# Expert stage of a streaming encoder trunk: gathered rows copied ahead of the tanh, the shared down-projection bank by bank, the last expert's products ahead of a weight conversion

## The chip, the cores and the metric

The kernel runs on one core of one Trainium2 chip. The metric is the device time of one execution in microseconds (us), the median over the runs. The core's engines work side by side, each through its own list of instructions in order: TensorE (PE: matrix products, with its weight loads as PEld), VectorE (DVE), ScalarE (ACT), GpSimd (POOL, almost unused here) and SyncE (SP, which issues the DMA transfers of the weights). They wait for one another by semaphores.

## The reference

Two layers of an encoder trunk run over 320 tokens (256 of a prompt, 64 of a sample), width 1024. What matters here is the second half of each layer, a mixture of experts; everything before it (attention, mLSTM, gated MLP, merge, first layer norm) is untouched.

```python
def _swiglu(x, wg, wu, wd):
    return (jax.nn.silu(x @ wg) * (x @ wu)) @ wd

def _moe(x, router_w, router_b, wg, wu, wd, sg, su, sd):
    ...                                   # s = sigmoid router; best group of 4 experts, best 2 in it
    out = _swiglu(xf, sg, su, sd)         # shared expert, all 320 tokens
    for e in range(N_EXPERTS):            # 16 experts, hidden width 256
        out = out + gate[:, e:e + 1] * _swiglu(xf, wg[e], wu[e], wd[e])
    return out
```

Each layer then ends with a layer norm of `DN_ALPHA * x + moe_out`. All values are f32.

## The kernel before

**Weights.** All weights come as blocks of 128 x 1024 f32 (512 KB), numbered through both layers. SP loads block n into one of 8 raw buffers (`w32`, L424). ACT rounds it to f16, `hi_at` (L545, writes `whi`), and DVE takes the rest, `lo_at` (L1034, writes `wlo`); both have 4 slots. So every product is made of three f16 products (whi by hi, whi by lo, wlo by hi), summed in PSUM. `hi_at(n)` waits until PE is done with block n-4 (`blk_done`), `lo_at(n)` waits for `hi_at(n)` (`hi_done`), PE's product waits for `lo_at(n)` (`ready`, `lo_done`), and SP's load of block n+8 waits for `lo_at(n)` as well.

**Expert stage.** The tokens of a group of 4 experts are gathered into 128 columns, so that an expert works on 128 columns and not on 320. For each of the 16 experts e (4 groups of 4; e2 is its parity) the engines do this, all written out by hand in this order:
- PE (L2190 to L2213): four blocks of 24 matmuls, j = 0 to 3 (gate half 0, up half 0, gate half 1, up half 1), into the banks `UPB[2*e2]` and `UPB[2*e2+1]`. After j = 0 come the two matmuls that spread the expert's gate values (L2137, L2139), after j = 1 come the 12 matmuls of `gather` (L2160) that fetch a quarter of the next group's rows into bank 5. UPB is the banks 1, 2, 3, 0 in this order, so even experts use 1 and 2, odd ones 3 and 0.
- ACT (L945 to L961): `hi_e(1)`, `hi_e(2)`, tanh of the gate halves (L950), `hi_e(3)`, the copy of the gathered rows out of bank 5 into `x_grp` (L955), `hi_e(4)`, and the f16 rounding of the hidden values (L960), which waits for DVE's products of this expert (`e_prod`). `hi_e(j)` converts block g0+3+j, where g0 is the expert's first block.
- DVE (L1631 to L1652): `lo_e(1)`, `lo_e(2)`, `lo_e(3)`; then the three products: (1 + tanh) by gate (L1636, waits for the tanh), by up (L1640, frees the expert's two banks: `e_free`), by the expert's gate values (L1644, `e_prod`); then `lo_e(4)` and the low part of the hidden values (L1649, waits for L960, signals `e_lo`).

At a group's start PE makes a small product for the way back (L2190, bank 7), ahead of which it waits until the copies of the previous group's four gathers are done (`xg_ev`), and ACT copies its result (L936) ahead of `hi_e(1)`.

**Down stage.** Once the experts are done PE runs `down` (L2150) for the shared expert's first half of the output: 24 matmuls of 320 columns over banks 0, 1, 2, 3, after a wait for the last expert's `e_free`. Its signal `blk_done` lets ACT convert the fourth block after it. Then `group_down` (L2233) makes 24 matmuls of 512 columns for each of 4 groups; its first waits for the last expert's `e_lo`. `scatter` (L2249) brings the results back to token order, and the same follows for the output's second half.

Of the kernel before, what the change touches and what calls it, by code (L numbers as in the profile page):

```python
# [35 lines left out]
ACT = mybir.ActivationFunctionType  # L36
# [3 lines left out]
P = 128  # L40
DM, L = 1024, 2
TP, TS, PAST = 256, 64, 256
T = TP + TS
# [49 lines left out]
def slot(l, n):  # L93
    return (l * NB + n) % SLOTS
# [23 lines left out]
def build_trunk(nc, d):  # L118
    with ExitStack() as ctx:
# [416 lines left out]
        def _(act):  # L536
# [48 lines left out]
            for l in range(0, L):  # L585
# [331 lines left out]
                with act.If(fits):  # L917
# [14 lines left out]
                    for gg in range(0, GROUPS // 2):  # L932
                        for g2 in range(2):

                            act.wait_ge(ot_ps.sem, ot_ps.value(l, gg * 2 + (g2 + 1)))
                            A(slot_tok[:, bass.ds((gg * 2 + g2) * T, T)], bank[7][:, 0:T], ACT.Copy,  # L936
                              scale=1 / (UN * XS)).then_inc(ot_ev.sem, 1)
                            for qq in range(0, 2):
                                for e2 in range(2):
                                    e = gg * 8 + qq * 2 + (4 * g2 + e2)  # L940
                                    g0 = e * 4 + (U0 + 4)

                                    def hi_e(j):
                                        hi_at(l, g0 + (j + LEAD))

                                    hi_e(1)
                                    hi_e(2)
                                    act.wait_ge(blk_done.sem, blk_done.value(l, g0 + 3))
                                    act.wait_ge(e_free.sem, e_free.value(l, e))
                                    A(ht[:, 0:2 * CAP], bank[UPB[2 * e2]][:, 0:2 * CAP], ACT.Tanh,  # L950
                                      scale=UN / 2).then_inc(e_tanh.sem, 1)
                                    hi_e(3)

                                    act.wait_ge(xg_ps.sem, xg_ps.value(l, e + 5))
                                    A(f16_b[:, bass.ds(qq * 1024 + (e2 * 512 + HEND + (1 - g2) * 2048),  # L955
                                                       512)], bank[5][:, :], ACT.Copy
                                      ).then_inc(xg_ev.sem, 1)
                                    hi_e(4)
                                    act.wait_ge(e_prod.sem, e_prod.value(l, e + 1))
                                    A(hhi[:, bass.ds(e * (2 * CAP) + H0, 2 * CAP)], h2[:, 0:2 * CAP],  # L960
                                      ACT.Copy, scale=UN * UN * XS / (2 * GS)).then_inc(e_hi.sem, 1)  # L961
# [65 lines left out]
        def _(dve):  # L1027
# [82 lines left out]
            for l in range(0, L):  # L1110
# [500 lines left out]
                with dve.If(fits):  # L1611
# [11 lines left out]
                    for ee in range(0, EXPERTS // 2):  # L1623
                        for e2 in range(2):
# [3 lines left out]
                            def lo_e(j):  # L1628
                                lo_at(l, g0 + (j + LEAD))

                            lo_e(1)  # L1631
                            lo_e(2)
                            lo_e(3)

                            dve.wait_ge(e_tanh.sem, e_tanh.value(l, e + 1))
                            V.scalar_tensor_tensor(h1[:, 0:W2], ht[:, 0:W2], 1.0,  # L1636
# [7 lines left out]
                            V.tensor_tensor(two(h2[:, 0:W2]), two(h1[:, 0:W2]),  # L1644
                                            bank[4 + 2 * e2][:, 0:CAP].unsqueeze(1).broadcast_to(
                                                [P, 2, CAP]), ALU.mult).then_inc(e_prod.sem, 1)
                            lo_e(4)
                            dve.wait_ge(e_hi.sem, e_hi.value(l, e + 1))
                            V.scalar_tensor_tensor(hlo[:, bass.ds(e * W2 + H0, W2)], h2[:, 0:W2],  # L1649
# [59 lines left out]
        def _(pe):  # L1709
# [16 lines left out]
            def ready(l, n):  # L1726

                pe.wait_ge(lo_done.sem, lo_done.value(l, n + 1))
# [52 lines left out]
            for l in range(0, L):  # L1781
# [385 lines left out]
                with pe.If(fits):  # L2167
# [85 lines left out]
                                a.then_inc(sums.sem, 1)  # L2253

                    pe.wait_ge(u_lo.sem, u_lo.value(l, 2))
                    pe.wait_ge(e_free.sem, e_free.value(l, EXPERTS))
                    down(l, D0, slot(l, D0), half0, 0, True, False)
                    for gg in range(0, GROUPS // 2):
                        for g2 in range(2):
                            group_down(gg * 2 + g2, g2, 0)  # L2260
# [201 lines left out]
```

## Time and profile before

| | us |
|---|---|
| median of 3 runs | 1105.39 (1103.49 to 1106.1) |
| profiled execution, its own time | 1105.55 |
| span of that execution, first to last instruction | 1103.3 |
| PE busy | 1031.3 (93%) |
| DVE busy | 835.9 (76%) |
| ACT busy | 659.2 (60%) |
| mean granted TensorE clock | 0.984 |

The profile describes one execution. Busy times are sums over the whole span; a stage has its own limit, so the expert stage has to be read from its own stretch. It lies at about 375 to 487 us in the first layer and 919 to 1029 us in the second. A row of the timeline gives an instruction's start (us from the span's start) and duration; an instruction may start shortly before the one ahead of it on its engine has ended. In square brackets stands how long the engine was idle before it and what ended that.

### The profile page before, as it was taken

The numbers are of one execution on the slowest core, as the hardware profiler recorded it, in microseconds if no ns is written. First come the engines' busy times: TensorE is split into PE (matmuls) and PEld (weight loads), VectorE is DVE, ScalarE is ACT, GpSimd is POOL, SyncE is SP. The second block draws the span as 40 slices with busy tenths as digits, with TensorE's granted clock in tenths as the row PEclk, the third lists the DMA queues.
The fourth block names the chain that finished last, engine by engine and source line by source line (L and its number), as shares of the span: only waits on it lengthen the run. The fifth ranks groups of instructions, "written<-read, shape, count | busy, mean of one in ns | idle before, by whom it ended". The sixth has DMA issues, their size and how long they took to land. (4 is left out here: it accounts for less than half of the span.)

```text
span 1103.3 us, 24810 instructions
## 1 busy us (share of the span) xinstructions
PE 1031.3 (93%) x10206; PEld 790.6 (72%) x10206; DVE 835.9 (76%) x1500; ACT 659.2 (60%) x1059; POOL 0.7 (0%) x10
## 2 busy tenths in 40 slices
PE   6999999999998799999999999999999888999994
PEld 4877777777775699965467777777777567999442
DVE  4786768654878699988987766676559777999886
ACT  5655545654345777777667445556533567777763
POOL 0000000000000000000000000000000000000000
PEclk9999999999999899999999999999999999999998
DMA  9744343323552389988725433442243415999861
GB/s 350 274 151 156 123 155 118 115 97 124 191 167 75 114 294 324 333 305 305 267 89 190 151 129 136 139 140 93 97 152 136 147 46 166 329 329 326 322 230 50
DMA packets 59655, 205.08 MB, mean 186 GB/s; under 512 B 7088, under 2 KB 10348, under 8 KB 59020
## 3 DMA queue, kind: packets, MB, share of 16 engines
q1 hardware_dynamic: 55980, 195.96, 51.2%
q10 hardware_dynamic: 3552, 7.42, 1.9%
q8 instruction: 85, 1.39, 0.5%
q14 instruction: 38, 0.31, 0.1%
HBM read 198.77 MB, written 3.40 MB: 183 GB/s over the span
## 5 line engine op out<-in xcount | busy, mean ns | idle before, releaser
L1034 DVE SCALAR_TENSOR_TENSOR wlo<-w,whi 128x1024 f16<-128x1024 f32 x358 | 429.7, 1221 | 83.5 <-ACT whi L545 81.9
L545 ACT ACTIVATE whi<-w 128x1024 f16<-128x1024 f32 x358 | 370.3, 1049 | 81.8 <-PE bank L1718 51.3
L1718 PE MATMUL bank<-xhi,whi 128*128 128x320 f16 x704 | 211.3, 300 | 0.0
L1718 PE MATMUL bank<-xlo,whi 128*128 128x320 f16 x704 | 210.8, 299 | 0.0
L1718 PE MATMUL bank<-xhi,wlo 128*128 128x320 f16 x704 | 210.7, 299 | 0.0
L1718 PE MATMUL bank<-arena_b,whi 128*128 128x128 f16 x2048 | 181.0, 220 | 0.0
L1718 PE MATMUL bank<-arena_b,wlo 128*128 128x128 f16 x1024 | 176.8, 220 | 0.0
L1718 PEld LDWEIGHTS bank<-arena_b,whi 128*128 128x128 f16 x2048 | 158.4, 98 | 0.0
L1718 PEld LDWEIGHTS bank<-arena_b,wlo 128*128 128x128 f16 x1024 | 100.8, 98 | 0.0
L1718 PEld LDWEIGHTS bank<-xhi,whi 128*128 128x128 f16 x704 | 68.9, 98 | 30.5 <-issue 2.5
L1718 PEld LDWEIGHTS bank<-xhi,wlo 128*128 128x128 f16 x704 | 69.0, 98 | 26.9
L1718 PEld LDWEIGHTS bank<-xlo,whi 128*128 128x128 f16 x704 | 69.0, 98 | 26.3 <-issue 1.4
L1741 PE MATMUL bank<-whi,xhi 128*128 128x128 f16 (+1 forms) x384 | 66.4, 220 | 0.0
L1741 PE MATMUL bank<-wlo,xhi 128*128 128x128 f16 (+1 forms) x384 | 66.0, 219 | 0.0
L1741 PE MATMUL bank<-whi,xlo 128*128 128x128 f16 (+1 forms) x384 | 66.0, 219 | 0.0
L1718 PE MATMUL bank<-br_hi,whi 128*128 128x320 f16 x192 | 57.4, 299 | 0.0
L1718 PE MATMUL bank<-br_lo,whi 128*128 128x320 f16 x192 | 57.4, 299 | 0.0
L1718 PE MATMUL bank<-br_hi,wlo 128*128 128x320 f16 x192 | 57.4, 299 | 0.0
L2233 PE MATMUL bank<-whi,arena_a 128*128 128x512 f16 x128 | 48.6, 379 | 1.8 <-DVE wlo L1034 1.8
L2233 PE MATMUL bank<-wlo,arena_a 128*128 128x512 f16 x128 | 48.5, 379 | 0.0
L2233 PE MATMUL bank<-whi,arena_b 128*128 128x512 f16 x128 | 48.5, 379 | 0.0
L689 ACT ACTIVATE arena_a<-bank,par_h 128x320 f32<-128x320 f32 x24 | 12.7, 527 | 58.6 <-PE bank L1718 58.6
(353 smaller groups left out, 1770.8 us busy)
## 6 DMA issues: line engine op xcount, KB each, us to landing
w<-in_w SPq DMA_DIRECT2D x358, 512.0 KB, 4.7
arena_b<-head_rows ACTq DMA_DIRECT2D x2, 1920.0 KB, 7.7
xT<-in_x SPq DMA_DIRECT2D x2, 640.0 KB, 4.8
out_y<-xT SPq DMA_DIRECT2D x4, 320.0 KB
rows<-in_rows ACTq DMA_DIRECT2D x1, 1024.0 KB, 11.4
rows<-in_rows SPq DMA_DIRECT2D x1, 1024.0 KB, 5.8
out_ckv<-arena_a SPq DMA_DIRECT2D x2, 320.0 KB
acc<-kr SPq DMA_DIRECT2D x2, 288.0 KB
```

The lines of the kernel that those rows point to most:

```text
L545: A(whi[:, n % SLOTS, :], w32[:, n % RAW, :], ACT.Copy, scale=WS).then_inc(hi_done.sem, 1)
L689: A(dst, bank[(M0 + step) % 4][:, 0:T], func, scale=scale, bias=par_t[:, bass.ds(col, 1)]).then_inc(z_ev.sem, 1)
L1034: V.scalar_tensor_tensor(wlo[:, n % SLOTS, :], w32[:, n % RAW, :], WS, whi[:, n % SLOTS, :], ALU.mult, ALU.subtract).then_inc(lo_done.sem, 1)
L1718: ins = M(out, w[:, s, sub * P:(sub + 1) * P], rhs(part, k), start=(n == 0), stop=(n == 3 * len(subs) - 1))
L1741: ins = M(bank[b][0:m, i * P:(i + 1) * P], x[:, k, t0:t0 + m], w[:, s, k * P:(k + 1) * P], start=(j == 0), stop=(j == 3 * KD - 1))
L2233: a = M(b[:, :], h_[:, bass.ds(g * (8 * CAP) + ((2 * q + kt) * CAP + H0), CAP)], w[:, slot(l, n), kt * 512:(kt + 1) * 512], start=(q == 0 ...
```

## The change

Three edits, all in the branch where every group's tokens fit into 128 columns (the one that runs here):
- ACT: the copy of the gathered rows (L955) moves from behind `hi_e(3)` to ahead of the tanh (L950), for each of the 16 experts.
- DVE: for the last expert only, `lo_e(3)` moves from ahead of the three products to behind them.
- PE: the shared expert's first `down` starts after a wait for the free banks of expert 14 only, does all six matmuls of bank 1, then of bank 2, then waits for the last expert's `e_free` and does banks 3 and 0. It was both halves of the depth over banks 0, 1, 2, 3. The 24 products are the same.

```diff
@@ -945,16 +945,15 @@
 
                                     hi_e(1)
                                     hi_e(2)
+                                    act.wait_ge(xg_ps.sem, xg_ps.value(l, e + 5))
+                                    A(f16_b[:, bass.ds(qq * 1024 + (e2 * 512 + HEND + (1 - g2) * 2048),
+                                                       512)], bank[5][:, :], ACT.Copy
+                                      ).then_inc(xg_ev.sem, 1)
                                     act.wait_ge(blk_done.sem, blk_done.value(l, g0 + 3))
                                     act.wait_ge(e_free.sem, e_free.value(l, e))
                                     A(ht[:, 0:2 * CAP], bank[UPB[2 * e2]][:, 0:2 * CAP], ACT.Tanh,
                                       scale=UN / 2).then_inc(e_tanh.sem, 1)
                                     hi_e(3)
-
-                                    act.wait_ge(xg_ps.sem, xg_ps.value(l, e + 5))
-                                    A(f16_b[:, bass.ds(qq * 1024 + (e2 * 512 + HEND + (1 - g2) * 2048),
-                                                       512)], bank[5][:, :], ACT.Copy
-                                      ).then_inc(xg_ev.sem, 1)
                                     hi_e(4)
                                     act.wait_ge(e_prod.sem, e_prod.value(l, e + 1))
                                     A(hhi[:, bass.ds(e * (2 * CAP) + H0, 2 * CAP)], h2[:, 0:2 * CAP],
@@ -1630,7 +1629,8 @@
 
                             lo_e(1)
                             lo_e(2)
-                            lo_e(3)
+                            if e < EXPERTS - 1:
+                                lo_e(3)
 
                             dve.wait_ge(e_tanh.sem, e_tanh.value(l, e + 1))
                             V.scalar_tensor_tensor(h1[:, 0:W2], ht[:, 0:W2], 1.0,
@@ -1644,6 +1644,8 @@
                             V.tensor_tensor(two(h2[:, 0:W2]), two(h1[:, 0:W2]),
                                             bank[4 + 2 * e2][:, 0:CAP].unsqueeze(1).broadcast_to(
                                                 [P, 2, CAP]), ALU.mult).then_inc(e_prod.sem, 1)
+                            if e == EXPERTS - 1:
+                                lo_e(3)
                             lo_e(4)
                             dve.wait_ge(e_hi.sem, e_hi.value(l, e + 1))
                             V.scalar_tensor_tensor(hlo[:, bass.ds(e * W2 + H0, W2)], h2[:, 0:W2],
@@ -2253,8 +2255,17 @@
                                 a.then_inc(sums.sem, 1)
 
                     pe.wait_ge(u_lo.sem, u_lo.value(l, 2))
-                    pe.wait_ge(e_free.sem, e_free.value(l, EXPERTS))
-                    down(l, D0, slot(l, D0), half0, 0, True, False)
+                    pe.wait_ge(e_free.sem, e_free.value(l, EXPERTS - 1))
+                    ready(l, D0)
+                    for b in UPB:
+                        if b == UPB[2]:
+                            pe.wait_ge(e_free.sem, e_free.value(l, EXPERTS))
+                        for kt in range(2):
+                            for w, h_ in ((whi, hhi), (whi, hlo), (wlo, hhi)):
+                                a = M(bank[b][:, 0:T], w[:, slot(l, D0), (4 * kt + b) * P:(4 * kt + b + 1) * P],
+                                      h_[:, kt * T:(kt + 1) * T], start=(kt == 0 and w is whi and h_ is hhi),
+                                      stop=False)
+                    a.then_inc(blk_done.sem, 1)
                     for gg in range(0, GROUPS // 2):
                         for g2 in range(2):
                             group_down(gg * 2 + g2, g2, 0)
```

ACT, a group's first expert, before. `bank7` is the small product's, `bank1` the gate halves' and `bank5` the gather's; `whi<-w32` are the conversions `hi_e`:

```order
L936 ACTIVATE arena_a<-bank7 128x320 [waits ot_ps]
L545 ACTIVATE whi<-w32 128x1024 [waits blk_done,loaded5]
L545 ACTIVATE whi<-w32 128x1024 [waits blk_done,loaded6]
L950 ACTIVATE mq<-bank1 128x256 [waits e_free,blk_done]
L545 ACTIVATE whi<-w32 128x1024 [waits blk_done,loaded7]
L955 ACTIVATE arena_b<-bank5 128x512 [waits xg_ps]
L545 ACTIVATE whi<-w32 128x1024 [waits blk_done,loaded0]
L960 ACTIVATE arena_a<-mo 128x256 [waits e_prod]
```

And now:

```order
L936 ACTIVATE arena_a<-bank7 128x320 [waits ot_ps]
L545 ACTIVATE whi<-w32 128x1024 [waits blk_done,loaded5]
L545 ACTIVATE whi<-w32 128x1024 [waits blk_done,loaded6]
L949 ACTIVATE arena_b<-bank5 128x512 [waits xg_ps]
L954 ACTIVATE mq<-bank1 128x256 [waits e_free,blk_done]
L545 ACTIVATE whi<-w32 128x1024 [waits blk_done,loaded7]
L545 ACTIVATE whi<-w32 128x1024 [waits blk_done,loaded0]
L959 ACTIVATE arena_a<-mo 128x256 [waits e_prod]
```

The copy out of bank5 stands ahead of the tanh, and two conversions now stand in a row behind the tanh. It is so for all 16 experts.

DVE, the last expert, from the last product of expert 14 on, before (`wlo<-w32,whi` are the conversions `lo_e`, x3 three in a row):

```order
L1644 TENSOR_TENSOR mo<-mk,bank4 128x256 [waits gb_ps]
L1034 SCALAR_TENSOR_TENSOR wlo<-w32,whi 128x1024 [waits hi_done]
L1649 SCALAR_TENSOR_TENSOR arena_b<-mo,arena_a 128x256 [waits e_hi]
L1034 SCALAR_TENSOR_TENSOR wlo<-w32,whi 128x1024 [waits hi_done] x3
L1636 SCALAR_TENSOR_TENSOR mk<-mq,bank3 128x256 [waits e_tanh]
L1640 TENSOR_TENSOR mk<-mk,bank0 128x256 [waits blk_done]
L1644 TENSOR_TENSOR mo<-mk,bank6 128x256 [waits gb_ps]
L1034 SCALAR_TENSOR_TENSOR wlo<-w32,whi 128x1024 [waits hi_done]
L1649 SCALAR_TENSOR_TENSOR arena_b<-mo,arena_a 128x256 [waits e_hi]
```

And now:

```order
L1644 TENSOR_TENSOR mo<-mk,bank4 128x256 [waits gb_ps]
L1033 SCALAR_TENSOR_TENSOR wlo<-w32,whi 128x1024 [waits hi_done]
L1651 SCALAR_TENSOR_TENSOR arena_b<-mo,arena_a 128x256 [waits e_hi]
L1033 SCALAR_TENSOR_TENSOR wlo<-w32,whi 128x1024 [waits hi_done] x2
L1636 SCALAR_TENSOR_TENSOR mk<-mq,bank3 128x256 [waits e_tanh]
L1640 TENSOR_TENSOR mk<-mk,bank0 128x256 [waits blk_done]
L1644 TENSOR_TENSOR mo<-mk,bank6 128x256 [waits gb_ps]
L1033 SCALAR_TENSOR_TENSOR wlo<-w32,whi 128x1024 [waits hi_done] x2
L1651 SCALAR_TENSOR_TENSOR arena_b<-mo,arena_a 128x256 [waits e_hi]
```

One conversion has moved from the three ahead of the products to the one behind them; the low part of the hidden values is still last.

PE, the first product of the shared down-projection, from its first matmul on, before:

```order
L2150 MATMUL bank0<-arena_a,whi 128x320 [waits lo_done,e_free,u_lo]
L2150 MATMUL bank0<-arena_b,whi 128x320
L2150 MATMUL bank0<-arena_a,wlo 128x320
L2150 MATMUL bank1<-arena_a,whi 128x320
L2150 MATMUL bank1<-arena_b,whi 128x320
L2150 MATMUL bank1<-arena_a,wlo 128x320
L2150 MATMUL bank2<-arena_a,whi 128x320
L2150 MATMUL bank2<-arena_b,whi 128x320
L2150 MATMUL bank2<-arena_a,wlo 128x320
```

And now, with the rows that only repeat left out:

```order
L2265 MATMUL bank1<-arena_a,whi 128x320 [waits lo_done,e_free,u_lo]
L2265 MATMUL bank1<-arena_b,whi 128x320
L2265 MATMUL bank1<-arena_a,wlo 128x320
L2265 MATMUL bank1<-arena_a,whi 128x320
...
L2265 MATMUL bank2<-arena_a,whi 128x320
...
L2265 MATMUL bank3<-arena_a,whi 128x320 [waits e_free]
...
L2265 MATMUL bank3<-arena_a,wlo 128x320
```

The wait for `e_free` is for one expert fewer at the first matmul, and a second one stands at bank3, twelve matmuls later.

## Rows read from the trace of the kernel before

**Rows 1.** Waits over the whole span: total us, times, longest us.

```profile
PE bank L2190 <- ACT arena_b L955: 5.5, 6, 0.9
...
PE bank L2150 <- issue: 5.2, 2, 2.6
```

**Rows 2.** Stretches: us, busy time of each engine, PEclk, DMA share, GB/s.

```profile
375.90:382.40 6.50, 5.12 (x50) 4.86 (x48) 4.03 (x7) 3.74 (x5) 0.00 (x0) 0.50 0.35 96
404.50:430.30 25.80, 24.87 (x443) 24.73 (x444) 24.54 (x33) 20.27 (x30) 0.00 (x0) 1.00 0.93 329
481.00:487.00 6.00, 3.41 (x25) 2.47 (x26) 4.30 (x7) 2.14 (x4) 0.00 (x0) 1.00 0.89 320
487.00:508.00 21.00, 21.00 (x101) 9.61 (x99) 19.60 (x19) 18.26 (x20) 0.00 (x0) 1.00 0.87 326
```

**Rows 3.** Timeline of DVE, expert 1 of the first layer.

```profile
389.23 3.50 DVE L1034 SCALAR_TENSOR_TENSOR wlo<-w,whi 128x1024 f16<-128x1024 f32 x3
392.65 0.41 DVE L1636 SCALAR_TENSOR_TENSOR mk<-mq,bank 128x256 f32<-128x256 f32 x1
...
393.65 0.42 DVE L1644 TENSOR_TENSOR mo<-mk,bank 128x256 f32<-128x256 f32 x1
393.99 1.22 DVE L1034 SCALAR_TENSOR_TENSOR wlo<-w,whi 128x1024 f16<-128x1024 f32 x1
```

**Rows 4.** Timeline of ACT, same expert, until its hidden values are rounded.

```profile
387.84 0.42 ACT L960 ACTIVATE arena_a<-mo 128x256 f16<-128x256 f32 x1 [1.20 <-DVE mo L1644]
388.16 1.99 ACT L545 ACTIVATE whi<-w 128x1024 f16<-128x1024 f32 x2
390.05 0.36 ACT L950 ACTIVATE mq<-bank 128x256 f32<-128x256 f32 x1
390.32 1.05 ACT L545 ACTIVATE whi<-w 128x1024 f16<-128x1024 f32 x1
391.26 0.58 ACT L955 ACTIVATE arena_b<-bank 128x512 f16<-128x512 f32 x1
391.74 1.05 ACT L545 ACTIVATE whi<-w 128x1024 f16<-128x1024 f32 x1
394.10 0.42 ACT L960 ACTIVATE arena_a<-mo 128x256 f16<-128x256 f32 x1 [1.31 <-DVE mo L1644]
```

**Rows 5.** All instructions of line 1636, the first product of each expert, both layers.

```profile
L1636 DVE SCALAR_TENSOR_TENSOR mk<-mq,bank x32: 410/414/416, 386.4 to 1025.1; 128x256 f32<-128x256 f32 x32
```

**Rows 6.** Timeline of ACT, tanh of the first layer's first expert.

```profile
383.88 0.38 ACT L950 ACTIVATE mq<-bank 128x256 f32<-128x256 f32 x1 [1.75 <-PE bank L1718]
```

**Rows 7.** Timeline of ACT at the start of the second group (expert 4).

```profile
406.95 0.42 ACT L936 ACTIVATE arena_a<-bank 128x320 f16<-128x320 f32 x1
407.27 1.99 ACT L545 ACTIVATE whi<-w 128x1024 f16<-128x1024 f32 x2
409.66 0.38 ACT L950 ACTIVATE mq<-bank 128x256 f32<-128x256 f32 x1 [0.40 <-PE bank L1718]
```

**Rows 8.** Timeline of DVE, third low conversion of expert 4.

```profile
411.02 1.23 DVE L1034 SCALAR_TENSOR_TENSOR wlo<-w,whi 128x1024 f16<-128x1024 f32 x1 [0.31 <-ACT whi L545]
```

**Rows 9.** Timeline of DVE, end of expert 14 and expert 15, first layer.

```profile
475.17 1.22 DVE L1034 SCALAR_TENSOR_TENSOR wlo<-w,whi 128x1024 f16<-128x1024 f32 x1
476.31 0.41 DVE L1636 SCALAR_TENSOR_TENSOR mk<-mq,bank 128x256 f32<-128x256 f32 x1
...
483.06 0.42 DVE L1640 TENSOR_TENSOR mk<-mk,bank 128x256 f32<-128x256 f32 x1
...
485.05 0.42 DVE L1649 SCALAR_TENSOR_TENSOR arena_b<-mo,arena_a 128x256 f16<-128x256 f32 x1
```

**Rows 10.** Timeline of PE, first matmul of the shared product and of group_down.

```profile
483.59 0.30 PE L2150 MATMUL bank<-arena_a,whi 128*128 128x320 f16 x1 [2.59 <-issue]
...
486.84 0.38 PE L2233 MATMUL bank<-whi,arena_a 128*128 128x512 f16 x1
```

**Rows 11.** Issues of weight loads at 481 to 487 us: count, KB, median us to landing.

```profile
w<-in_w SPq DMA_DIRECT2D x3, 512.0 KB, 5.8
```

## Prediction, made before the changed kernel ran

> **What bounds the kernel now.** I read the waits first. PE, busy for 93% of the span, waits at each group's start for the copy of the last gather, 0.9 us each, 5.5 us in all six times, and 2.6 us in each layer ahead of the shared down product [rows 1]. Those are the waits that the three edits aim at, some 10.7 us in all. Whether they can be had depends on what paces the stretch between them, so I then read the stretches: over one group's 25.8 us PE is busy 24.87 us and DVE 24.54 us, ACT 20.27 us [rows 2]. PE and DVE are too close to be told apart by busy time, and PE's own work of at most 24.87 / 4 = 6.22 us per expert has to be held against DVE's order of work. So I went to DVE's timeline of one inner expert. Its first product starts at 392.65 [rows 3], that of the expert ahead at 386.4 [rows 5]: 6.27 us apart, and DVE never waits. The pieces fill it: three low conversions from 389.23 on, 1.14 us apart, products, the fourth conversion at 393.99. So **DVE sets the pace** inside a group at 6.27 us per expert, PE keeps up with a little to spare, and PE's 0.9 us at a group's start is partly that slack.
>
> ACT has idle time too, but it lies in one place: 1.31 us ahead of the rounding of the hidden values, where it waits for DVE's last product [rows 4]. Between that rounding and the third conversion ACT doesn't stop: rounding at 387.84, two conversions from 388.16, tanh at 390.05, third conversion from 390.32 to 391.37. DVE's third low conversion needs that result. The three end at 389.23 + 3.50 = 392.73, so the third starts 1.22 us earlier, at 391.51 [rows 3]. How soon after its release it can start is seen at expert 4: the tanh starts at 409.66, the conversion behind it 0.27 us later and ends after 1.05, at 410.98 [rows 4, 7], and DVE starts at 411.02 [rows 8], so 0.03 us. **The slack between ACT's third conversion and DVE's is therefore 391.51 - 391.37 - 0.03 = 0.11 us.** This is the number on which the prediction rests.
>
> **Edit 1, the copy ahead of the tanh.** It adds no work, but puts the copy on the way from the rounding to the third conversion. What it costs there is its distance to the next instruction on ACT, 391.26 to 391.74, 0.48 us [rows 4]. 0.11 us of that is covered; 0.37 us is not. And the delay isn't paid once: DVE's product then comes later, ACT's rounding waits for it and starts its next round later. The ring, from an expert's last product (L1644) to that of the next: product to rounding 0.45 [rows 3, 4], rounding to first conversion 0.32, two conversions to the next instruction 1.89, copy 0.48, tanh to third conversion 0.27, the conversion 1.05 [rows 4], release 0.03, third low conversion to first product 1.14 (475.17 to 476.31 [rows 9]), first to last product 1.00 (392.65 to 393.65 [rows 3]). Sum **6.63 us**; without the copy it was 6.15, under DVE's 6.27, and hence hidden. Every piece is an instruction in order on its engine or a wait for a result, so no slack elsewhere shortens it. PE with 6.22 us can't be the bound of it, and now waits for `lo_done` some 0.4 us per expert.
>
> Two places differ. The first expert of a layer isn't delayed: its tanh waits 1.75 us for PE [rows 6] and the copy goes into that wait. A group's first expert (three in a layer) has L936 in the ring as well, 406.95 to 407.27, 0.32 us [rows 7], so 6.95 us. Before it took (476.31 - 386.38 - 11 x 6.27) / 3 = 6.99 us [rows 5, 9], since there the tanh waited 0.40 us for PE [rows 7], which had waited for the copy. So what edit 1 is made for is worth 0.04 us at each of three places in a layer, and its cost of 0.36 us is paid at eleven. The first product of expert 14 comes at 386.38 + 11 x 6.63 + 3 x 6.95 = 480.16 in place of 476.31: **+3.85 us per layer**.
>
> **Edit 2, the third low conversion of expert 15 behind the products.** The first product starts 1.14 us earlier in relation to expert 14: 480.16 + 6.27 - 1.14 = 485.29. The tanh allows that: last product of expert 14 at 481.16, plus 0.45 + 0.32 + 1.89 + 0.48, tanh from 484.30 to 484.66. `e_free` comes with the end of the second product, 0.49 + 0.42 us later, at 486.20. But the low part of the hidden values (L1649) stays last on DVE, behind the same instructions as before; only their order has changed: 485.05 [rows 9] + 3.85 = 488.90, ending at 489.32. The moved conversion is block D0 + 2 (the third of the down stage); SP's load of the block 8 further on waits for it, and goes out at about 487.9. ACT needs it once PE is done with block D0 + 6, six blocks of six matmuls into `group_down`, which runs some 101 matmuls in 21.0 us [rows 2]: about 7.5 us after 489.4, so 9 us later, and such loads take 5.8 us [rows 11]. ACT's rounding comes at 486.74, in time. Nobody waits for the rest.
>
> **Edit 3, the shared product bank by bank.** Twelve of its matmuls can run before `e_free`. All 24 took 486.84 - 483.59 = 3.25 us [rows 10], twelve take 1.63. So the second half runs from 486.31 to 487.94, where PE would otherwise have ended at 486.31 + 3.25 = 489.56. `group_down` then waits for `e_lo`: 489.32 + 0.11 (the latency of 483.06 + 0.42 to 483.59 [rows 9, 10]) = **489.43**. So **`e_lo` is next in line** and takes nearly all of what this edit frees: about 1.5 us of PE idle time ahead of L2233. Before, `group_down` started at 486.84 [rows 10].
>
> **The sum.** 489.43 - 486.84 = +2.59 us in each layer; the copy by itself would give, by the same steps, a first product at 486.79 and `group_down` at 491.06, +4.22, and the two other edits give back 1.63. By themselves they would gain 486.84 - 485.58 = 1.26 us. Behind it PE is busy for all of the next 21.0 us [rows 2], so the shift is handed on whole. The second layer runs at the same pace (last first product at 1025.1 [rows 5]). 2 x 2.59 = 5.2 us; the profiled execution took 1105.55 us (1103.3 between first and last instruction), which is 0.16 above the median. **1105.55 + 5.2 = 1110.7 us.**
>
> **Bounds of what the trace doesn't show.** No row has the copy ahead of a tanh. If its whole duration of 0.58 us counted, that is 0.10 x 14 experts x 2 = 2.8 us more: 1113.5. The cheapest neighbour that reads PSUM and is no smaller than the tanh is L936 with 0.32 us: 0.16 x 14 x 2 = 4.5 us less, 1106.2. I take 0.48, the same instruction, and don't go the whole way down in the range. Edits 2 and 3 return between 0 and 1.63 us a layer.
>
> **Rivals.**
> (a) *The copy finds cover and PE's waits go.* Then DVE's 6.27 holds at all experts: 3 x 0.72 at the groups' starts and 1.26 at the end, 3.4 us a layer, **1098.7 us**. For it speaks that PE's waits are real and sit on its engine; against it the 0.11 us. It decides at a slack of 0.48. The Trainium skill, Perfetto Trace Analysis, section Optimization Strategies, says that the goal is to keep the matrix engine as busy as possible and that one should work on the engines that block it. By that rule this change is the right one and this rival would come true; the trace has the blocking engine right, but the place wrong. 5 in 100.
> (b) *TensorE's clock falls.* PE would get a wait of 0.4 us at each expert. After 2 us of idling the clock was 0.50 over 375.9 to 382.4, the lower of its two levels, 1.2 GHz; in a group with some 0.9 us of waits and over 481 to 487 with 2.6 us it stayed at 1.00, 2.4 GHz [rows 2]. A stretch like the first loses 3 us of PE's work, one per layer: **1117 us**. The Trainium skill, TensorE: Matmul & The Clock Gate, section A second HAM failure mode: psum-queue depth-cycling, reports a kernel whose frequent short PE idles made the clock oscillate. That would be this case; the trace so far speaks against it. 3 in 100.
> (c) *The delay is largely made good*: the cheap copy of above, or a gain at the groups' starts larger than 0.04: **1105 to 1106.5 us**. The ring would have to be wrong by 0.16 us or more. 6 in 100.
> (d) *The change doesn't do what it says at the end*: the early half of the shared product gains nothing and edit 2 neither, since something other than `e_free` holds PE: 4.22 x 2, **1114 us**. 6 in 100.
>
> **How the numbers follow.** The forecast and its bounds have 80 in 100. The range 1107.3 to 1114.3 holds these and (d); outside are (a), (b) and (c), 14 in 100. A measurement of this kernel can tell about 0.2% (2.2 us) from no change. Slower by more than that: forecast, (b) and (d), and little of (c): 0.90. Within it: most of (c), 0.05. Faster: (a), 0.05.
>
> **What the new profile would show.** First products of inner experts 6.63 us apart, at a group's start 6.95; a wait of DVE of about 0.36 us for ACT's conversion at each of them; no wait of L2190 for the copy; twelve matmuls of the shared product, a short wait, twelve more, then about 1.5 us of PE idle ahead of the first L2233 (now L2235), released by DVE's low part; that first one at about 489.4 us. Wrong would be: a distance of 6.27, or a DVE that doesn't wait for ACT at the third low conversion.

## The result, and the profile after

The changed kernel took **1109.62 us**, the median of five runs (1109.27 to 1111.36); the kernel before took 1104.32 us in five runs (1103.49 to 1106.10) on the same chip. The ratio is 1.0047, with a 95% interval of 1.0033 to 1.0062. The profiled execution took 1109.62 us as well, 1107.5 of it between the first and the last instruction. The prediction was 1110.7 us.

To see where the time went, I measure the expert stage of a layer from its first gather matmul (L2190, in the changed kernel L2192) to the first matmul of `group_down`. Before, it took 112.17 and 109.98 us in the two layers; the first of the two holds a stretch of 6.5 us at the lower clock, 1.2 GHz [rows 2], which the other hasn't. After, it took 112.78 and 112.77 us. The undisturbed stages give **+2.79 us per layer**; what lies ahead of the first stage (374.67 before, 375.08 after), between the two (432.54, 432.87) and behind the second (73.94, 74.00) grew by 0.8 us in sum. These parts, which the edits don't touch, vary as much by themselves: what lies ahead of the first stage takes 373.98 us in experiment 1 and 375.38 in experiment 2. Two layers are 5.6 us; the two spans are only 4.2 apart because the execution profiled before paid 112.17 - 109.98 = 2.2 us for its stretch at 1.2 GHz and the one after did not: 5.6 - 2.2 + 0.8 = 4.2.

The first products of all experts, after (the counterpart of [rows 5]; columns: durations in ns, first and last start):

```profile
L1636 DVE SCALAR_TENSOR_TENSOR mk<-mq,bank x32: 412/414/417, 384.6 to 1029.4; 128x256 f32<-128x256 f32 x32
```

The last one starts at 1029.4 in place of 1025.1. Singly, the first ones start at 384.62, 391.26, 397.91, 404.55 and 411.52: 6.64, 6.65 and 6.64 us apart inside a group and 6.97 at the start of the next, in place of 6.27 and 6.99. ACT's and DVE's timelines of expert 1, after (start, duration, engine, line, idle time ahead and its releaser), show why:

```profile
386.07 0.42 ACT L959 ACTIVATE arena_a<-mo 128x256 f16<-128x256 f32 x1 [1.50 <-DVE mo L1644]
386.39 1.99 ACT L545 ACTIVATE whi<-w 128x1024 f16<-128x1024 f32 x2
388.29 0.58 ACT L949 ACTIVATE arena_b<-bank 128x512 f16<-128x512 f32 x1
388.77 0.37 ACT L954 ACTIVATE mq<-bank 128x256 f32<-128x256 f32 x1
389.03 2.00 ACT L545 ACTIVATE whi<-w 128x1024 f16<-128x1024 f32 x2
392.72 0.42 ACT L959 ACTIVATE arena_a<-mo 128x256 f16<-128x256 f32 x1 [1.69 <-DVE mo L1644]
```

```profile
387.47 2.36 DVE L1033 SCALAR_TENSOR_TENSOR wlo<-w,whi 128x1024 f16<-128x1024 f32 x2
390.12 1.22 DVE L1033 SCALAR_TENSOR_TENSOR wlo<-w,whi 128x1024 f16<-128x1024 f32 x1 [0.29 <-ACT whi L545]
391.26 0.41 DVE L1636 SCALAR_TENSOR_TENSOR mk<-mq,bank 128x256 f32<-128x256 f32 x1
391.75 0.42 DVE L1640 TENSOR_TENSOR mk<-mk,bank 128x256 f32<-128x256 f32 x1
392.26 0.42 DVE L1644 TENSOR_TENSOR mo<-mk,bank 128x256 f32<-128x256 f32 x1
```

The copy stands 0.48 us (388.29 to 388.77) ahead of the tanh, where [rows 4] has none; DVE, which had no wait of that length there [rows 3], now waits 0.29 us for the third conversion. ACT's own wait has grown from 1.31 to 1.69 us: its work wasn't lengthened, it was put on the way of a ring, and the time came out as idle time elsewhere on the same engine. Rounding to rounding is 392.72 - 386.07 = 6.65 us.

The end of the stage on PE, after (the counterpart of [rows 10]), the wait of L2192 at the start of the second group (its counterpart is in [rows 1]), and the stretches that answer to [rows 2] (length, busy time of PE, weight loads, DVE, ACT, POOL, then the granted clock):

```profile
402.30 0.30 PE L2192 MATMUL bank<-mats,arena_a 128*128 128x128 f16 x3 [0.27 <-ACT arena_b L949]
...
482.86 0.30 PE L2265 MATMUL bank<-arena_a,whi 128*128 128x320 f16 x1
...
484.74 0.31 PE L2265 MATMUL bank<-arena_a,whi 128*128 128x320 f16 x1
...
487.86 0.39 PE L2235 MATMUL bank<-whi,arena_a 128*128 128x512 f16 x1 [1.32 <-DVE arena_b L1651]
```

```profile
404.00:430.00 26.00, 24.96 (x428) 23.79 (x426) 24.18 (x32) 19.26 (x29) 0.00 (x0) 1.00 0.93 317
482.00:488.00 6.00, 4.50 (x39) 2.90 (x37) 5.83 (x9) 4.53 (x7) 0.00 (x0) 1.00 0.88 296
488.00:509.00 21.00, 21.00 (x100) 9.58 (x99) 19.30 (x19) 17.20 (x19) 0.00 (x0) 1.00 0.93 347
```

PE's 0.9 us at the groups' starts has become 0.27 at all six, and its 2.6 us ahead of the shared product is gone: twelve matmuls from 482.86, twelve more from 484.74. In its place stands a wait of 1.32 us ahead of `group_down`, for the low part of the hidden values. So the edits removed the waits that they aimed at, and the stage got longer.

### The profile page after: what moved, and what is told of

Read it like the earlier page. It is cut to its first block and busy times, and to the rows that moved or that the text cites. A ratio compares the mean times of both kernels' runs of the same rounds, so it can differ in the third digit from the quotient of the medians.

```text
span 1107.5 us, 24810 instructions
## 1 busy us (share of the span) xinstructions
PE 1037.3 (94%) x10206; PEld 788.2 (71%) x10206; DVE 837.9 (76%) x1500; ACT 659.6 (60%) x1059; POOL 0.7 (0%) x10
## 5 line engine op out<-in xcount | busy, mean ns | idle before, releaser
L1720 PE MATMUL bank<-arena_b,whi 128*128 128x128 f16 x2048 | 183.5, 219 | 4.5 <-DVE wlo L1033 2.0
L1720 PEld LDWEIGHTS bank<-arena_b,whi 128*128 128x128 f16 x2048 | 155.8, 98 | 10.7 <-issue 6.0
L2235 PE MATMUL bank<-whi,arena_a 128*128 128x512 f16 x128 | 48.6, 380 | 4.5 <-DVE arena_b L1651 2.6
L2235 PE MATMUL bank<-wlo,arena_a 128*128 128x512 f16 x128 | 48.5, 379 | 0.0
L2235 PE MATMUL bank<-whi,arena_b 128*128 128x512 f16 x128 | 48.5, 379 | 0.0
```

Source lines behind the costliest of these rows:

```text
L1720: ins = M(out, w[:, s, sub * P:(sub + 1) * P], rhs(part, k), start=(n == 0), stop=(n == 3 * len(subs) - 1))
L2235: a = M(b[:, :], h_[:, bass.ds(g * (8 * CAP) + ((2 * q + kt) * CAP + H0), CAP)], w[:, slot(l, n), kt * 512:(kt + 1) * 512], start=(q == 0 ...
```

## The experiments

Ten kernels, in three lots, each beside runs of the kernel before on the same chip, whose median was 1105.36 us beside experiments 1, 2, 3 and 5, 1105.19 beside 4, 6, 7 and 8, and 1105.65 beside 9 and 10. Experiments 4, 7 and 8 are single runs without a ratio; what is read of them is their trace. Stage times are those of the first and second layer, in us. My theory is the ring through ACT and DVE; its rivals are a cost on PE (its clock, or bank waits) and a cost of the edits at the end.

**1. The copy alone.** Edit 1 put into the kernel before:

```diff
 hi_e(1)
 hi_e(2)
+act.wait_ge(xg_ps.sem, xg_ps.value(l, e + 5))
+A(f16_b[...512], bank[5][:, :], ACT.Copy).then_inc(xg_ev.sem, 1)
 act.wait_ge(blk_done.sem, blk_done.value(l, g0 + 3))
 act.wait_ge(e_free.sem, e_free.value(l, e))
 A(ht[...], ..., ACT.Tanh, ...).then_inc(e_tanh.sem, 1)
 hi_e(3)
-act.wait_ge(xg_ps.sem, xg_ps.value(l, e + 5))
-A(f16_b[...512], bank[5][:, :], ACT.Copy).then_inc(xg_ev.sem, 1)
 hi_e(4)
```

> Edit 1 alone, on the kernel before: the copy of the gathered rows ahead of the tanh; the end of the stage as before. Theory (a ring between DVE and ACT of 6.65 us that takes the place of DVE's 6.27): first products of inner experts 6.65 us apart, 6.97 at a group's start, first product of expert 15 about 4.4 us later in relation to that of expert 0, group_down too; both layers 8.8 us, so about 1.0080 times the kernel before. Rival (PE's waits are the cost, the loss lies in the two other edits): faster than before by up to 5.4 us, 0.995. Rival (the lag is paid once in a group): about 1.001.

1116.66 us (four runs), 1.0098 of before (1.0066 to 1.0129). Stages 116.03 and 116.10. The pace is 6.64 to 6.65, 6.97 at a group's start, so the ring is there without the other edits. But it accounts for only part: the stage is 6.1 us longer than 109.98 and my steps had 4.22. The rest is at its end (PE's timeline, then stretches):

```profile
485.14 0.42 PE L2149 MATMUL bank<-arena_a,whi 128*128 128x320 f16 x1 [3.52 <-DVE mk L1639]
```

```profile
485.20:488.60 3.40, 3.40 (x14) 1.90 (x15) 1.82 (x3) 0.42 (x1) 0.00 (x0) 0.52 0.95 337
488.60:509.00 20.40, 20.40 (x101) 9.61 (x99) 17.44 (x17) 16.52 (x18) 0.00 (x0) 1.00 0.78 280
```

PE idled for 3.52 us ahead of the shared product, and the clock was 0.52 behind it, about the lower level of 1.2 GHz: 14 matmuls in 3.4 us, where experiment 8 has 25 in 3.3. The same happened in the second layer.

**2. The edits of the end alone.** Edits 2 and 3 in the kernel before, nothing of edit 1.

> Edits 2 and 3 alone, on the kernel before: the third low conversion of expert 15 behind the products and the shared product bank by bank; the copy stays behind the third conversion. Theory: pace 6.27 us and 7.0 at a group's start as before, from the first product of expert 0 to the first matmul of group_down 99.2 us in place of 100.45 (1.26 less), so 2.5 us less in all, ratio 0.9977. Rival (the loss comes from the end of the stage): 1.002 or more. Rival (nothing there is on the path): 1.000.

1100.62 us (eleven runs), 0.9953 (0.9939 to 0.9967): faster, and by more than the 0.9977 that was forecast. Stages 108.83 and 108.76, so 1.2 us less than 109.98 in each (forecast 1.26); pace 6.26 to 6.27 inside a group, as before. `group_down` waits as forecast, PE's timeline:

```profile
484.21 0.39 PE L2235 MATMUL bank<-whi,arena_a 128*128 128x512 f16 x1 [1.25 <-DVE arena_b L1651]
```

The cost is all edit 1's. But 2 x 1.2 us is 2.4, and the runs gained 4.7; experiments 9 and 10 come back to that.

**3. The third low conversion behind the products, everywhere.** If the ring is what costs, taking a piece out of it must bring the loss back. In the changed kernel:

```diff
 lo_e(1)
 lo_e(2)
-if e < EXPERTS - 1:
-    lo_e(3)
 ...
-if e == EXPERTS - 1:
-    lo_e(3)
+lo_e(3)
 lo_e(4)
```

> The changed kernel with one thing more: the third low conversion stands behind the three products for all 16 experts, not for the last alone. The copy stays ahead of the tanh. Theory: it takes ACT's third conversion out of the ring, which is then 0.45 + 0.32 + 1.89 + 0.48 + 0.40 + 1.00 = 4.54 us, so DVE's own 6.27 us holds at all experts, at a group's start too; no wait of DVE for ACT's third conversion; group_down starts 3.9 us earlier than before in each layer, ratio 0.993, about 1096.5 us. Rival (the early copy costs by itself, through the tanh or through contention on ACT's or PSUM's side): pace stays at 6.6 us, ratio 1.004 as in the changed kernel. Rival (PE sets the pace once its waits are gone): 6.2 us and the same ratio of 0.993, but then PE doesn't wait and DVE does.

1093.27 us (four runs), 0.9885 (0.9854 to 0.9916). Stages 105.18 and 105.17, 7.6 us less than after, with the copy still ahead of the tanh. That is more than was forecast (0.993, from DVE's 6.27 us). Timelines of DVE and ACT, then PE's (the first gate-row matmul of experts 2, 3 and 4, and the end of the stage), and a stretch:

```profile
388.33 0.41 DVE L1634 SCALAR_TENSOR_TENSOR mk<-mq,bank 128x256 f32<-128x256 f32 x1
...
389.67 2.35 DVE L1033 SCALAR_TENSOR_TENSOR wlo<-w,whi 128x1024 f16<-128x1024 f32 x2
391.94 0.42 DVE L1648 SCALAR_TENSOR_TENSOR arena_b<-mo,arena_a 128x256 f16<-128x256 f32 x1
392.28 2.35 DVE L1033 SCALAR_TENSOR_TENSOR wlo<-w,whi 128x1024 f16<-128x1024 f32 x2
394.55 0.41 DVE L1634 SCALAR_TENSOR_TENSOR mk<-mq,bank 128x256 f32<-128x256 f32 x1
```

```profile
390.15 1.06 ACT L545 ACTIVATE whi<-w 128x1024 f16<-128x1024 f32 x1
```

```profile
389.89 0.22 PE L2136 MATMUL bank<-arena_a,exp_sel 128*128 128x128 f16 x1
...
396.03 0.22 PE L2136 MATMUL bank<-arena_a,exp_sel 128*128 128x128 f16 x1
...
402.31 0.22 PE L2136 MATMUL bank<-arena_a,exp_sel 128*128 128x128 f16 x1
...
479.42 0.39 PE L2232 MATMUL bank<-whi,arena_a 128*128 128x512 f16 x1 [1.04 <-DVE arena_b L1648]
```

```profile
400.00:426.00 26.00, 26.00 (x470) 26.00 (x468) 25.33 (x34) 22.71 (x32) 0.00 (x0) 1.00 0.97 337
```

The pace is 394.55 - 388.33 = 6.22 us, at the groups' starts too. PE is busy for all of 26 us and DVE doesn't wait either. PE's own pace is a little shorter, 396.03 - 389.89 = 6.14 us inside a group and 6.28 over a group's start (402.31 - 396.03), and the stage ends with PE waiting 1.04 us for DVE's low part. So 6.22 is what DVE's instructions take back to back.

That also corrects the reading of before, where the pace was 6.27. There DVE's low part and its next conversion started 0.37 us apart (DVE's timeline of before):

```profile
388.86 0.42 DVE L1649 SCALAR_TENSOR_TENSOR arena_b<-mo,arena_a 128x256 f16<-128x256 f32 x1
```

In experiment 3 it is 392.28 - 391.94 = 0.34. In before ACT's first conversion ends at 388.16 + 1.05 = 389.21 [rows 4] and DVE starts its own at 389.23 [rows 3]; in experiment 3 ACT's had ended at 391.21, 1 us ahead. So DVE did wait in before, for some 0.04 us, and 6.27 was a ring as well, through ACT's first conversion: 0.45 + 0.32 + 1.05 + 0.02 + 3.42 + 1.00 = 6.26 us [rows 3, 4].

PE's waits at the groups' starts are gone. Whether the copy has to stand ahead of the tanh for that, once the third low conversion stands behind the products, wasn't run.

**4. The changed kernel without edit 3**: the shared product in one piece, behind the wait for all experts.

> The changed kernel without edit 3 (edits 1 and 2; the shared product waits for the last expert's e_free and runs as before). Theory (e_lo is next in line): group_down starts about 0.2 us later than in the changed kernel in relation to the stage's start, 112.95 in place of 112.78 us, if the clock stays at 1.00; the shared product starts after some 2 us of PE idling and takes 3.25 us. Rival (the split product is worth its 1.6 us): 114.4 us.

One run, 1111.04 us. Stages 114.57 and 112.96. Both layers wait for the same 2.01 us, and the clock fell in one of them (PE's timeline, then stretches of the two layers):

```profile
484.22 0.30 PE L2152 MATMUL bank<-arena_a,whi 128*128 128x320 f16 x1 [2.01 <-DVE mk L1640]
```

```profile
484.20:489.00 4.80, 4.78 (x23) 2.94 (x24) 3.03 (x4) 0.71 (x2) 0.00 (x0) 0.64 0.93 317
1029.90:1034.90 5.00, 3.21 (x24) 2.36 (x25) 4.64 (x7) 2.48 (x4) 0.00 (x0) 1.00 0.92 297
```

At 2.4 GHz edit 3 is worth 112.96 - 112.77 = 0.19 us. Against the layer in which the clock fell it is 1.8. The split also keeps PE from idling in one piece, and in the changed kernel's two layers the clock didn't fall; but without the split it fell in only one of two, so that the split prevents it is likely and not shown.

**5. Half a copy ahead of the tanh.** In the kernel before, the copy of 512 columns as two of 256, one on each side:

```diff
+A(f16_b[... first 256], bank[5][:, 0:256], ACT.Copy)
 A(ht[...], ..., ACT.Tanh, ...).then_inc(e_tanh.sem, 1)
 hi_e(3)
-A(f16_b[...512], bank[5][:, :], ACT.Copy).then_inc(xg_ev.sem, 1)
+A(f16_b[... last 256], bank[5][:, 256:512], ACT.Copy).then_inc(xg_ev.sem, 1)
```

> On the kernel before: the copy in two halves of 256 columns, one ahead of the tanh, one behind the third conversion. Theory: a copy of 256 columns costs the ring its distance to the next instruction, some 0.27 us (as for the tanh), of which 0.11 is slack: pace 6.15 + 0.27 = 6.42 to 6.45 us in place of 6.27, at 11 experts of a layer; some 1.9 us per layer, ratio 1.003 to 1.004. Rival (the place of the signal for PE matters, not ACT's time): as before, 1.000. Rival (any instruction ahead of the tanh costs the same): pace 6.65 as with the whole copy.

1110.91 us (ten runs), 1.0050 (1.0034 to 1.0067), where 1.003 to 1.004 was forecast. Pace 6.43 us, as forecast. ACT's timeline has the half 0.27 us ahead of the tanh:

```profile
394.69 0.36 ACT L949 ACTIVATE arena_b<-bank 128x256 f16<-128x256 f32 x1
394.96 0.38 ACT L953 ACTIVATE mq<-bank 128x256 f32<-128x256 f32 x1
```

0.27 less the 0.11 of slack is 0.16, and 6.27 + 0.16 = 6.43: the ring takes from the dose what exceeds the slack, no more. Stages 112.95 and 113.27, 3.0 and 3.3 us more than before where 1.9 was forecast; as with the whole copy, PE's last wait had grown (to 3.08 and 3.07 us) and the clock fell behind it in both layers.

**6. The low part of the last hidden values first.** Experiment 3 leaves `group_down` waiting for the low part, as the changed kernel does. So, in experiment 3's kernel, for the last expert only:

```diff
-lo_e(3)
-lo_e(4)
+if e < EXPERTS - 1:
+    lo_e(3)
+    lo_e(4)
 dve.wait_ge(e_hi.sem, e_hi.value(l, e + 1))
 V.scalar_tensor_tensor(hlo[...], h2[...], ...).then_inc(e_lo.sem, 1)
+if e == EXPERTS - 1:
+    lo_e(3)
+    lo_e(4)
```

> A version for speed: the copy ahead of the tanh, the third low conversion behind the products for all experts, the split shared product, and for the last expert the low part of the hidden values ahead of the third and fourth low conversions, so that e_lo comes 1.7 us earlier. Theory: group_down then waits for the shared product (which ends at about 1.2 us before its present start), stage 103.95 us in place of 105.17, 109.98 before: 2 x 6.0 = 12 us less than before with both layers at full clock, ratio 0.986 to 0.989. Rival (the delayed conversions make group_down wait instead, or the weight loads that wait for them come late): stage as in the third experiment, 105.2, or a later end of the down stage, ratio as there.

**1090.45 us** (1089.36 to 1091.24, four runs), 0.9865 (0.9849 to 0.9882): the fastest of all, 1.35% ahead of the kernel before and, by the two ratios, 1.8% ahead of the changed one. Stages 104.16 and 103.98. DVE now waits a little for ACT's rounding, and `group_down` for nobody (timelines of DVE and PE):

```profile
477.50 0.43 DVE L1649 SCALAR_TENSOR_TENSOR arena_b<-mo,arena_a 128x256 f16<-128x256 f32 x1 [0.48 <-ACT arena_a L959]
```

```profile
478.29 0.30 PE L2266 MATMUL bank<-arena_a,wlo 128*128 128x320 f16 x1
478.42 0.38 PE L2236 MATMUL bank<-whi,arena_a 128*128 128x512 f16 x1
```

**7. The changed kernel without edit 2**: the third low conversion of the last expert back ahead of its products.

> The changed kernel without edit 2 (edits 1 and 3; the third low conversion stays ahead of the products for all experts). Theory: 113.15 us from the stage's start to group_down, 0.4 more than the changed kernel; the shared product comes in two halves, so no PE idle time of over 3 us, and the clock stays at 1.00, where the copy alone had a drop to half and 116.1 us. Rival (the clock drop belongs to the late e_free, whatever PE does ahead of it): drop again and over 114.5 us.

One run, 1109.14 us. Stages 113.10 and 113.11, clock 1.00 at the start of `group_down`. The second half of the shared product now waits, and `group_down` hardly does:

```profile
485.53 0.31 PE L2262 MATMUL bank<-arena_a,whi 128*128 128x320 f16 x1 [1.59 <-DVE mk L1639]
...
487.51 0.39 PE L2232 MATMUL bank<-whi,arena_a 128*128 128x512 f16 x1 [0.18 <-DVE arena_b L1648]
```

With edit 3 present, edit 2 is worth 0.33 us a layer. The two edits overlap: either gives the larger part, and both end at the low part of the hidden values.

**8. The copy alone, with PE kept busy.** To tell the clock from everything else at the stage's end: experiment 1 with 14 matmuls into a bank that nobody reads at that time, placed in PE's wait.

```diff
 pe.wait_ge(u_lo.sem, u_lo.value(l, 2))
+pe.wait_ge(ot_ev.sem, ot_ev.value(l, GROUPS))
+unread(7, 14)
 pe.wait_ge(e_free.sem, e_free.value(l, EXPERTS))
```

> Edit 1 alone with 14 matmuls of 320 columns into a bank that nobody reads, put into PE's 3.5 us wait ahead of the shared product. They change no result. Theory (in the run of edit 1 alone the clock fell because PE idled for 3.5 us, and this, not the wait itself, made up the 1.6 us by which group_down came later than the ring explains): clock 1.00 throughout the shared product, 24 matmuls in 3.25 us, stage 114.4 us in place of 116.1. Rival (the drop comes by a fixed pattern in time, or from the load of the stage): 116.1 again.

One run, 1112.05 us. Stages 114.39 and 114.48 in place of 116.03 and 116.10. PE's timeline and the stretch behind the wait:

```profile
481.57 2.06 PE L1748 MATMUL bank<-exp_sel,mats 128*128 128x320 f16 x14
485.21 0.31 PE L2149 MATMUL bank<-arena_a,whi 128*128 128x320 f16 x1 [1.58 <-DVE mk L1639]
```

```profile
485.20:488.50 3.30, 3.29 (x25) 2.38 (x26) 1.89 (x3) 0.42 (x1) 0.00 (x0) 1.00 0.92 359
```

The shared product starts at the same time, 485.21 against 485.14 (111.1 and 111.2 us behind the stage's start), and runs at 1.00. So the clock cost 1.6 us a layer in experiment 1, and the copy by itself costs 114.4 - 110.0 = 4.4 to 4.5 us.

**9. The kernel before, with PE kept busy.** The same three lines, in the kernel before.

> The kernel before, with 14 matmuls of 320 columns into a bank that nobody reads in PE's 2.6 us wait ahead of the shared product; nothing else is changed. Open is why edits 2 and 3 alone gave 0.47% (5.2 us) where their steps in the traces are 2 x 1.2 us. Theory: in a part of its executions the kernel before has a clock drop there, in one layer or in both, which the profiled execution didn't have, and edit 3 takes that away; then the filler alone gives up to 1.6 us per layer in part of the executions, ratio 0.997 to 0.999, and the trace is as before (stage 110.0 us). Rival (the rest of the 5.2 us comes from elsewhere, such as the clock at the first expert): 1.000.

1103.65 us (twelve runs) against 1105.65 (seventeen), ratio 0.9978 (0.9968 to 0.9988). Stages 109.94 and 109.94, the same as the undisturbed one of the profiled execution of before. So the filler changes nothing there, and yet the median fell by 0.2%. The mean granted clocks of the runs differ too, 0.9868 with the filler and 0.9843 without. A stretch of 3.4 us at half clock takes 3.4 x 0.5 / 1103 = 0.0015 off that mean, so the difference is one or two such stretches in an execution. That they lie behind the wait of 2.6 us, as my theory has it, fits the 1.6 us that such a stretch cost in experiment 1, but isn't shown: the mean doesn't tell the place. In the two traces the clock differs at another one, around the first expert, where the execution of before was at half clock in both layers, inside the stage of the first [rows 2] and ahead of that of the second, and this one in neither (stretches of this run, then of before):

```profile
370.50:383.00 12.50, 8.76 (x136) 7.51 (x134) 8.79 (x14) 7.34 (x13) 0.00 (x0) 1.00 0.36 122
914.00:926.00 12.00, 8.25 (x128) 7.17 (x127) 8.28 (x14) 7.60 (x13) 0.00 (x0) 1.00 0.38 118
```

```profile
915.10:918.50 3.40, 3.40 (x21) 1.88 (x19) 2.70 (x6) 0.70 (x2) 0.00 (x0) 0.50 0.37 113
```

The 1.9 us between the two profiled executions (1105.55 and 1103.61 us) are about the 2.2 us of that first stage.

**10. Edit 2 alone**, in the kernel before.

> Edit 2 alone on the kernel before: the third low conversion of expert 15 behind the products, the shared product whole. Theory: e_free comes 1.14 us earlier, the shared product with it; stage 108.9 us in place of 109.98, 0.1 more than with edit 3 as well; PE's wait there is 1.5 us, so no clock drop either, and the ratio that of edits 2 and 3 together, 0.995 to 0.996. Rival (edit 3 carries the gain): 0.998 or more.

1101.38 us (six runs), 0.9952 (0.9939 to 0.9966), the same as edits 2 and 3 together. PE's wait ahead of the shared product is 1.45 us in place of 2.59, and the stage of the first layer 108.84. That of the second is 110.68, and its clock is that of the first layer before [rows 2], at the first expert, ahead of all that the edits touch:

```profile
917.10:923.50 6.40, 5.70 (x55) 5.44 (x53) 4.25 (x6) 3.39 (x5) 0.00 (x0) 0.50 0.23 77
```

This bears on what experiment 2 left over. The steps in the trace give 2 x 1.2 us; the medians differ by 4.3 and 4.7 us, and the rest is about the 2.0 to 2.4 of experiment 9 (two medians, or the ratio). A possible reason is that the clock falls less often behind PE's wait once that is shorter; it isn't shown, since only one execution of each kernel has a trace, and in these the clock differs at the first expert and not behind the wait.

## Why the prediction was right, step by step

**The slack and the ring.** Right, and it carried the result. The prediction's ring was 6.63 us, measured 6.64 to 6.65; at a group's start 6.95, measured 6.97. Experiment 5 shows that 0.11 us of slack is the number: 256 columns cost 0.16, 512 columns 0.37 to 0.38. Experiment 3 shows that the ring is a ring: with one piece out of it the loss is gone and the pace drops to 6.22.

**What set the pace before.** Here the reading was off by 0.05 us. The prediction said that DVE never waits and sets the pace by its own 6.27 us; its own is 6.22, and it waited some 0.04 us for ACT's first conversion (experiment 3). The forecast doesn't suffer, since the 0.11 us were measured against the pace as it was. But ACT was in the way of the pace before any edit. The 0.05 us at some fourteen experts are also 0.7 of the 0.9 us by which experiment 3 gained more than forecast, 4.8 us a layer in place of 3.9.

**The copy's price.** 0.48 us was the right choice among the neighbours: the same 0.48 stands in ACT's timeline. Neither its duration of 0.58 nor the 0.32 of L936 counts.

**The sum of edit 1.** 4.22 us a layer, measured 4.4 to 4.5 at 2.4 GHz (experiment 8). The difference is the 0.015 to 0.02 us by which each of fourteen steps was set too low; that is also what is left between +2.59 and +2.79 a layer for the whole change. One of the readings shows it: the release was set at 0.03 us, and the rows give 411.02 - 410.98 = 0.04.

**Edits 2 and 3.** Together behind edit 1 they return 4.4 to 4.5 less 2.79, 1.65 us (forecast 1.63), by themselves 1.2 (1.26). That `e_lo` is next in line is right: 1.32 us of PE idle ahead of L2235, released by DVE's low part, where about 1.5 was said; and the first matmul of `group_down` came at 487.86, where 489.43 was said. That time was counted on in a stage that held the 2.2 us of the lower clock; less these, plus 0.41 by which the stage after started later and 0.20 for the ring, it is 487.84. That edit 3 is all but worthless is right at one clock level only (0.19 us). The step left out a likely second effect: it splits PE's idle time.

**What it got wrong.** "No wait of L2190 for the copy": one of 0.27 us stands at each of the six groups' starts. It lies beside the ring: the first products there are 6.97 us apart, the 6.95 forecast and the 0.02 by which every round was set too low. DVE's wait was put at 0.36 us and is shown as 0.29; the conversion itself is late by the 0.37 of the ring.

**The rivals.** (a) needed a slack of 0.48 us and found 0.11. By the Trainium skill, Perfetto Trace Analysis, section Optimization Strategies, one works on the engines that block the matrix engine; here the blocking engine was the right one and the copy still the wrong piece to move, since PE's waits of 0.9 us were slack against DVE's pace. (b), the clock, didn't come true in the changed kernel: it stayed at 1.00 with PE idling a little at every expert. The Trainium skill, TensorE: Matmul & The Clock Gate, section A second HAM failure mode: psum-queue depth-cycling, reports a kernel in which frequent short idles made it oscillate; no expert stage here shows that. But the clock did fall in three variants (1, 4 and 5), and not by many short waits: it fell behind the one long wait of PE, which the delayed last product had lengthened to 3.52 and some 3.07 us in 1 and 5. In 4 it was 2.01 us, shorter than the 2.59 of before, and the clock fell in one layer only. I had given this 3 in 100 on the ground that 2.6 us had left the clock alone in the profiled execution; experiment 4 shows that one such execution was too little to say so. (c) and (d) are out: the ring wasn't shorter by 0.16 us, and the end gave what it should.

**The total.** 5.2 us forecast from 1105.55, measured 5.6 in the trace's undisturbed stages and 5.3 between the medians. The prediction missed the median by 1.1 us, and all of that is in its starting point: the profiled execution with its 1105.55 us, where the median of the kernel before came out at 1104.32. That 5.2 and 5.3 agree so closely is in part luck: the steps were 0.4 us short in sum, and between the two medians lies also what each kernel loses to the clock. In the kernel before the filler of experiment 9 took some 2 us away; what it would take from the changed one isn't known.

What stays open: when the clock falls. Behind PE's wait at the stage's end it fell in one layer and not in the other with 2.01 us, in neither with 2.59 in the profiled execution of before, in both with 3.07 and 3.52. So the length of the wait alone doesn't decide it, and I haven't found what does. It is open too why a stage sometimes has a slow stretch at its first expert (before, layer 1; experiment 10, layer 2) and sometimes not. The 2 us of idling that the prediction put ahead of it don't explain it: PE waits the same 2.03 us there in the changed kernel's second layer, and the clock stays at 1.00. In the changed kernel's first layer the clock was low as well, but from 371.1 to 374.5 us, ahead of the stage's start at 375.08.

## What to carry to other kernels

Before moving a step ahead on an engine with idle time, add up the ring that it lands in, from one result to the same result a round later, and hold it against the engine that sets the pace: the idle time may lie elsewhere in the ring, and 0.48 us put in where there is 0.11 us of slack is paid at every round. A wait too short for the profile to list (0.04 us here) can still close such a ring. Look then for a piece that can leave the ring (the third low conversion, 7.6 us a layer), since that is worth more than filling the waits that the ring causes. And where a change makes TensorE's one long wait longer or shorter, price it at both clock levels and from more than one execution.

## What the runs showed of the hardware that I had not expected

- PE's wait ahead of the shared product can cost more than its own length. Behind 3.52 us of idling the shared product ran at a granted clock of 0.52, the lower level of 1.2 GHz, and 1.6 us a layer was lost; 14 unread matmuls of 2.06 us in that wait kept it at 1.00.
- The same filler in the kernel before gained 0.2% (ratio 0.9978), though the profiled execution shows nothing to gain behind the wait: 109.98 and 109.94 us for the stage. At which place of the other executions it gained isn't shown.
- Short waits did nothing of the kind. With some 0.3 us of PE idle time per expert of 6.65 us (24.96 us busy of 26), the clock was 1.00 for the whole stage.
